# One matmul over the high and low parts of 240 tokens in five projections of a float32 hybrid decoder layer

## What is computed

```python
xn = rmsnorm(x, g1)
q, k, v, o, ig, fg, u, vb, ga, gb = split_in(xn @ w_in)
h, C, n, m = mlstm_branch(q, k * DK_A ** -0.5, v, ig, log_sigmoid(fg), C, n, m)   # chunks of 128
y_a = (sigmoid(o) * h) @ w_a
y_b = spatial_gate(gelu(u), rmsnorm(gelu(vb), g_v), w_s, b_s) @ w_b
x = x + (sigmoid(ga) * y_a + sigmoid(gb) * y_b) @ w_o
up = rmsnorm(x, g2) @ w_up
a, gval = split(causal_conv(up), 2)
x = x + (silu(a) * gval) @ w_down
y = rmsnorm(x, g_final)
```

## Time and profile before

| | |
|---|---|
| median of 3 runs | 938.73 us |
| range of the runs | 938.55 to 939.69 us |
| span of the profiled execution (first to last instruction) | 936.5 us |
| its own time beside the span | not listed apart; the median lies 2.2 us above the span |
| TensorE busy | 912.5 us, 97%, 7432 matmul records |
| weight loads busy | 900.9 us, 96% |
| VectorE busy | 524.1 us, 56% |
| ScalarE busy | 365.3 us, 39% |
| POOL busy | 136.6 us, 15% |
| mean DMA rate | 106 GB/s |

### The profile page before, as it was taken

How to read it: one execution, slowest core, us unless ns; L and a number is a source line. 1 busy time by engine, 2 the same in 40 slices (tenths; PEclk the granted TensorE clock), 3 DMA queues, 4 the chain that set the end, 5 groups by cost and what they waited for, 6 DMA issues and landing times.

```text
span 936.5 us, 19633 instructions
## 1 busy us (share of the span) xinstructions
PE 912.5 (97%) x7432; PEld 900.9 (96%) x7432; DVE 524.1 (56%) x802; ACT 365.3 (39%) x550; POOL 136.6 (15%) x180
## 2 busy tenths in 40 slices
PE   7999999999999999999999999999999999999993
PEld 6999999999999999999999999999999999999993
DVE  7874565453685444433335787777777777332234
ACT  5562333443783332322223344444444444222230
POOL 1842000002261111000005610000000000000002
PEclk9999999999999999999999999999999999999997
DMA  4312233124683112252224222222222223323212
GB/s 182 135 69 90 91 112 135 50 90 152 211 304 126 67 67 88 86 185 91 90 90 118 90 79 101 90 90 90 90 90 90 90 90 95 104 83 98 86 62 91
DMA packets 30008, 99.10 MB, mean 106 GB/s; under 512 B 4480, under 2 KB 6560, under 8 KB 29848
## 3 DMA queue, kind: packets, MB, share of 16 engines
q1 hardware_dynamic: 28528, 93.46, 28.2%
q0 software_dynamic: 1152, 4.66, 1.7%
q10 hardware_dynamic: 296, 0.55, 0.2%
HBM read 91.32 MB, written 7.34 MB: 105 GB/s over the span
## 4 chain that ended last, share of the span: by engine, by line
PE 88%; DVE 4%; POOLq 3%; issue 2%; DVEq 1%; DMA 1%; POOL 1%; ACT 0%; ACTq 0%
PE out L1286 81%; PE aux L1286 3%; PE trp L1286 2%; POOLq L1263 2%; DVE xl L780 1%; POOLq L1261 1%; PE trp L1315 1%; DVE wlo L738 1%; DVE y L1151 1%; DMA cwb<-in_conv_wb 0%; DMA gains<-in_gains 0%; PE aux L1421 0%; DVE ftmp L1147 0%; DVEq L831 0%; DVE mmax L816 0%
## 5 line engine op out<-in xcount | busy, mean ns | idle before, releaser
L738 DVE TENSOR_TENSOR wlo<-raw,whi 128x1024 fp32r<-128x1024 f32 (+1 forms) x149 | 187.1, 1256 | 226.1 <-ACT whi L408 225.9
L408 ACT ACTIVATE whi<-raw 128x1024 fp32r<-128x1024 f32 (+1 forms) x149 | 156.5, 1050 | 267.5 <-PE out L1286 265.7
L1286 PE MATMUL out<-xh,whi 128*128 128x260 f32 x864 | 178.9, 288 | 2.0 <-DVE wlo L738 2.0
L1286 PE MATMUL out<-xh,wlo 128*128 128x260 f32 x864 | 173.9, 283 | 0.0
L1286 PE MATMUL out<-xl,whi 128*128 128x260 f32 x864 | 173.7, 282 | 0.0
L1286 PE MATMUL out<-x2h,wlo 128*128 128x260 f32 x704 | 141.9, 283 | 0.0
L1286 PE MATMUL out<-x2h,whi 128*128 128x260 f32 x704 | 141.8, 282 | 0.0
L1286 PE MATMUL out<-x2l,whi 128*128 128x260 f32 x704 | 141.7, 283 | 0.0
L1286 PEld LDWEIGHTS out<-xh,whi 128*128 128x128 f32 x864 | 133.4, 188 | 2.9 <-DVE wlo L738 2.4
L1286 PEld LDWEIGHTS out<-xh,wlo 128*128 128x128 f32 x864 | 133.1, 188 | 0.0
L1286 PEld LDWEIGHTS out<-xl,whi 128*128 128x128 f32 x864 | 133.1, 188 | 0.0
(11 more groups left out here) (255 smaller groups left out, 1278.1 us busy)
## 6 DMA issues: line engine op xcount, KB each, us to landing
raw<-in_w_slots SPq DMA_DIRECT2D x125, 512.0 KB, 3.2
raw<-in_w_dn SPq DMA_DIRECT2D x16, 448.0 KB, 3.2
c_ring<-in_C_state SPq DMA_DIRECT2D x8, 512.0 KB, 4.6
row<-scratch SPq DMA_DIRECT2D x8, 512.0 KB, 5.4
out_C_sample<-c_ring SPq DMA_DIRECT2D x8, 512.0 KB, 3.9
raw<-in_w_dn SPq DMA_DIRECT2D x8, 512.0 KB, 3.6
xres<-in_x_all POOLq DMA_DIRECT2D x1, 2080.0 KB, 10.7
x<-in_x_all SPq DMA_DIRECT2D x3, 520.0 KB, 5.5
```

The costliest lines, as they stand in the source:

```text
L408: return act.activation(out, in_, func, **kw_)
L738: TT(wlo[p][:, 0:width], raw[p][:, 0:width], whi[p][:, 0:width].bitcast(F32), ALU.subtract)\
L1286: return pe.matmul(*a, **k)
```

## The change

In Q, K, V, WO and DN (`twin=True`) the high weights take the low and the high part of tokens 0 to 239 in one matmul of 480 columns. The low part's product so lands beside the high part's in the bank, not on it, and is added when the bank is emptied (`cross`). All tiles, the others too, now cut the tokens at 240, and put them so that the 520 results lie in one run across both banks. High and low parts get one tensor with a common stride for this. In Q, K and V ScalarE's copy signals `q_copied`, `k_copied` or `v_copied`; VectorE adds the crossed 240 columns and signals `evac`. In WO and DN VectorE does a second add after a drain. `mid` of K and V tiles moves from k = 3 to k = 5.

```diff
+CUT = 240
...
+        def tokens(bank):
+            return bank[:, :, :].rearrange("p a b -> p (a b)")[:, 512 - CUT:512 - CUT + TOK]
+        def cross(bank):
+            return bank[:, 0, 512 - 2 * CUT:512 - CUT]
...
-                A(both(qT[:, j, :]), out2(n)).then_inc(evac[n.c % 2], 1)
+                A(qT[:, j, :], out2(n)).then_inc(s_qc, 1)
...
-                A(both(ftmp[h % 2][:, :]), out2(n), scale=DK ** -0.5).then_inc(evac[n.c % 2], 1)
+                A(ftmp[h % 2][:, :], out2(n), scale=DK ** -0.5).then_inc(s_kc, 1)
...
+            def q_cross(j):
+                dve.wait_ge(s_qc, j + 1)
+                TT(qT[:, j, 0:CUT], cross(out_ps[(S_Q + j) % 2]), qT[:, j, 0:CUT], ALU.add).then_inc(evac[(S_Q + j) % 2], 1)
             low(At(S_Q + 2))
+            q_cross(0)
...
                 if h >= 1:
                     k_side(h - 1)
                 low(At(S_K + h + 2))
+                dve.wait_ge(s_kc, h + 1)
+                front = ftmp[h % 2][:, 0:CUT]
+                STT(front, cross(out_ps[(S_K + h) % 2]), DK ** -0.5, front, ALU.mult, ALU.add).then_inc(evac[(S_K + h) % 2], 1)
...
             low(At(S_V + 2))
+            v_cross(0, 0)
...
-                    TT(both(x1[:, j, :]), out2(n), both(xres[:, j, :]), ALU.add).then_inc(evac[n.c % 2], 1)
+                    TT(x1[:, j, :], out2(n), xres[:, j, :], ALU.add)
+                    dve.drain()
+                    TT(x1[:, j, 0:CUT], cross(out_ps[n.c % 2]), x1[:, j, 0:CUT], ALU.add).then_inc(evac[n.c % 2], 1)
                     dve.drain()
                     dve.nop().then_inc(s_x1, 1)
...
-                        TT(x1[:, j, h], o[:, a, :], x1[:, j, h], ALU.add).then_inc(s_x2f, 1)
+                        m = TT(x1[:, j, h], o[:, h], x1[:, j, h], ALU.add)
+                        if a == 0:
+                            dve.drain()
+                            m = TT(x1[:, j, 0:CUT], cross(out_ps[bank]), x1[:, j, 0:CUT], ALU.add)
+                        m.then_inc(s_x2f, 1)
...
-                    for wt, x in ((whi[p], hi), (whi[p], lo), (wlo[p], hi)):
-                        for a in range(2):
-                            m = MM(o[:, a, 0:HALF], wt[:, w], x[:, k0 + k, a * HALF:(a + 1) * HALF],
...
+                    if twin:
+                        MM(both_, whi[p][:, w], x[:, :, 0:CUT], start=first, stop=last, skip_group_check=True)
+                    else:
+                        MM(front, whi[p][:, w], hi[:, 0:CUT], start=first, stop=False)
+                        MM(front, whi[p][:, w], lo[:, 0:CUT], start=False, stop=False)
+                    MM(back, whi[p][:, w], hi[:, CUT:TOK], start=first, stop=False)
+                    MM(back, whi[p][:, w], lo[:, CUT:TOK], start=False, stop=False)
+                    MM(front, wlo[p][:, w], hi[:, 0:CUT], start=False, stop=last, skip_group_check=twin)
+                    m = MM(back, wlo[p][:, w], hi[:, CUT:TOK], start=False, stop=last)
...
-                tile(At(S_K + h), xh, xl, mid=(lambda: k_side(h - 1)) if h >= 1 else None)
+                tile(At(S_K + h), of(x_hl), twin=True, mid_at=5, mid=(lambda: k_side(h - 1)) if h >= 1 else None)
```

More of the change, by code:

```diff
@@ L1128, in dn_tile @@
                         h = slice(a * HALF, (a + 1) * HALF)
-                        TT(x1[:, j, h], o[:, a, :], x1[:, j, h], ALU.add).then_inc(s_x2f, 1)
+                        m = TT(x1[:, j, h], o[:, h], x1[:, j, h], ALU.add)
[3 more added lines that the diff above has]
+                        m.then_inc(s_x2f, 1)
                     return
-                TT(both(x1[:, j, :]), o, both(x1[:, j, :]), ALU.add).then_inc(evac[bank], 1)
+                TT(x1[:, j, :], o, x1[:, j, :], ALU.add)
+                dve.drain()
+                TT(x1[:, j, 0:CUT], cross(out_ps[bank]), x1[:, j, 0:CUT], ALU.add).then_inc(evac[bank], 1)
                 dve.drain()
@@ L1286, in MM, with tile @@
                 return pe.matmul(*a, **k)
-            def tile(n, hi, lo, k0=0, nk=KT, bank=None, use=None, start=True, stop=True, mid=None, mid_at=3, each=None, end=None):
+            def tile(n, hl, k0=0, nk=KT, bank=None, use=None, start=True, stop=True, mid=None, mid_at=3, each=None, end=None,
+                     twin=False):
                 p = n.c % 2
@@ L1293, in tile @@
                     pe.wait_ge(evac[p if bank is None else bank], n.half(1) if use is None else use)
-                o = out_ps[p if bank is None else bank]
+                b = out_ps[p if bank is None else bank]
+                both_ = b[:, 0, 512 - 2 * CUT:512].rearrange("p (a t) -> p a t", a=2)
+                front, back = b[:, 0, 512 - CUT:512], b[:, 1, 0:TOK - CUT]
                 for k in range(nk):
@@ L1326, in vb_tile @@
                 n = At(S_VB + t, i, 2)
-                tile(n, xh, xl, each=each, mid_at=5, mid=lambda: transposes(At(B_VB + t - 1, i, 2), n.plus(-1)))
-            tile(At(S_GATE), xuh, xul, each=s_xu)
-            tile(At(S_VB), xuh, xul)
+                tile(n, of(x_hl), each=each, mid_at=5, mid=lambda: transposes(At(B_VB + t - 1, i, 2), n.plus(-1)))
+            tile(At(S_GATE), of(xu_hl), each=s_xu)
+            tile(At(S_VB), of(xu_hl))
             pe.wait_ge(s_tri, 1)
-            tile(At(S_VB + 1), xuh, xul, end=lambda: transposes(At(B_VB), At(S_VB)))
+            tile(At(S_VB + 1), of(xu_hl), end=lambda: transposes(At(B_VB), At(S_VB)))
             vb_tile(1, 0, each=s_xn)
@@ L1446, in norm_sums @@
                 m.then_inc(signal, 1)
[L1448 to L1449 removed]
+            tile(At(S_UP), of(x2_hl), each=s_x2, mid_at=5, mid=lambda: norm_sums(s_acc, 1, s_ss2))
+            tile(At(S_UP + 1), of(x2_hl))
             with pe.Fori(1, FT) as i:
                 for t in range(2):
[L1452 removed]
+                    tile(At(S_UP + t, i, 2), of(x2_hl))
             def dn_pair(i, first=False):
@@ L1460, in dn_pair @@
                         pe.wait_ge(s_al, FT - 1 if q < 2 else FT)
-                    tile(n, acth, actl, k0=DN_CUTS[q], nk=DN_CUTS[q + 1] - DN_CUTS[q], bank=bank,
-                         use=At(S_DN + t, i, 2).half(1), start=q == 0, stop=q == 2)
+                    tile(n, act_of, k0=DN_CUTS[q], nk=DN_CUTS[q + 1] - DN_CUTS[q], bank=bank,
+                         use=At(S_DN + t, i, 2).half(1), start=q == 0, stop=q == 2, twin=True)
             dn_pair(0, True)
```

115 lines of the change are left out of this document (65 added, 50 removed).

## The result

The changed kernel takes **944.66 us** (median of 4 runs, 943.8 to 946.15), the kernel before, beside it, 938.99 (4 runs, 938.55 to 939.69): ratio **1.0064**, 95% interval 1.005 to 1.0078. It is slower by 5.7 us, where 931.0 was forecast and 943 was the upper end of the range. The profiled execution has a span of 942.1 us, 5.6 above that of before.

The account below looks back on a forecast made before the run. TensorE's matmul stream, busy 912.5 of 936.5 us, was taken as the bound. Terms -13.8 + 2.1 + 2.9 + 0.45 + 0.45 = -7.9 us gave 930.8 us, stated as 931; range 924 to 943 us, held at 0.80.

Parts of the forecast that it names:

- Step 1: Q, K, V, output projection and down: five matmuls for six in 368 k tiles, 37.5 ns each, -13.8 us.
- slow columns: Rival, all float32r matmuls: columns themselves cost 0.461 ns each, their count is unchanged, so nothing saved; 941.3 us, chance 0.12.
- the rival in which the change gives more: Rival, all tiles: 240 columns cost 111 ns, 25 us less, about 906 us; chance 0.05.
- Step 2: The other 808 k tiles, cut 240 and 280: 240 stays at 119.9 ns, 280 just at it; +2.1 us.
- third rival: Load and stream slow each other: 240 columns stay at 119.9 ns, 280 pay 128.2; 960 us, chance 0.15.
- Step 3: K and first V tiles: crossed add queued behind `low` makes TensorE wait 0.73 us in four rounds, +2.9 us.
- Steps 4 and 5: Second add after a drain, at output projection into up and at down's last tile: +0.45 us each.
- Step 6: Reads of 520 columns in one run instead of two, no DMA added or moved: costs nothing.

Follow-up runs that it names:

- the kernel at 256: The changed kernel with its tokens cut at 256 and 264 instead of 240 and 280, merged matmuls of 512 columns: 941.86 us, ratio 1.0031.

## Why the prediction was wrong

The spans' sum, step by step, from the stages' first starts:

| step | forecast, us | measured, us |
|---|---|---|
| 1. five matmuls for six, 368 k tiles | -13.8 | -1.7 (4.7 ns each) |
| 2. new cut, 808 k tiles | +2.1 | +3.4 (4.2 ns each) |
| 3. waits in K and V | +2.9 | +2.7 |
| 4. WO into up | +0.45 | +0.45 |
| 5. the end | +0.45 | +0.47 |
| sum | -7.9 | +5.3 (spans: +5.6) |

**Step 1 failed, by 12 of the 13.2 us: the price of one matmul by its width.** I read 119.9 ns as a floor of load and matmul and gave the 480 columns 202.3 ns; they take 218.1, and 240 take 112. The 11.6 ns above 108.3 were 7 to 8 ns of slow columns and 4 of a charge per matmul. The rival "slow columns" (0.461 ns each, 941.3 us) had the mechanism, and 221 ns for 480 columns was the nearest of my marks; it had no floor under it and so priced the new cut at nothing. The 111 ns for 240 columns of the rival in which the change gives more came true too, but beside 202.3 and 119.0 ns for the wide ones. The rows against the floor were at hand: eight passes of 128 columns start 111 ns apart with full weight loads, so a floor of 119.9 was no property of the load; and the last pair ahead of the transposes is as slow with a short load next, which I gave to the rival and then not its weight. My neighbours for long streams were passes of plain float32, which take 215/257 = 0.84 ns a column: they can't show a limit that lies at 0.446.

**Step 2** was mis-sized: a 240 does not stay at 119.9 but falls to the true floor of about 112 and no further, while a 280 pays 129.6. On a straight line the two would cancel; they are 1.4 ns a pair short of it. That is the third rival's shape (the narrow ones gain less than the wide ones pay), with a floor of 111.7 for 119.9 and a price of 4.2 for 25 ns a k tile. Its mark was a 240 of 112.9 ns with the 280 at 128.3; measured were some 112 and 129.6. About 1 of the 4.2 ns belongs to the order of the matmuls, which I costed at nothing.

**Step 3** was right in its loop, and its sum came out right by luck. Middle to middle is 8.72 us (8.71 forecast). But TensorE's own work there is 8 x 0.716 + 2.53 = 8.26 us, not 7.98, so a round loses 0.46, four lose 1.8; the other 0.9 us come from the V tile whose `low` POOL holds up, of which I had written that the chain is short from V1 on. That `low` of 3.19 us stands in the trace of before. That the waits are VectorE's order is shown: the add ahead of `low` takes them away, in K, then in V.

**Steps 4 and 5** hold: TensorE waits 0.5 us for POOL ahead of the norm sums where it waited for nothing, and the end is 0.47 us longer.

**Step 6** holds as far as it was tried: two pieces are free, and the placement in one run changes nothing. But the order into the banks, which I didn't cost, is worth 1.5 us at 260 columns in the medians (937.19 against 938.66 beside it) and 2.3 from the first tile on.

The range had a slip of its own: 5 us below 930.8 is 925.8, not 924. Nothing hangs on it, as the result lies above the upper end.

The Trainium skill's rule ("TensorE: Matmul & The Clock Gate", section "Back-to-back issue gap": N / 2.4 + 2.5 ns), which the page calls the gap of an isolated matmul, made the change worth 0.9 us at the most and came nearer to a saved matmul's worth (2.5 ns, an estimate by that rule, against 4.7) than my 37.5 did. Its figure for a column does not hold in this stream: 232.9 ns for 512 float32r columns, where it gives 215.8.

## What to carry to other kernels

Find out what a matmul's time consists of before merging matmuls: two matmuls above the floor save only the charge per instruction (here 4 ns of 120 by the line, 1 to 2 ns a k tile in the kernel at 256), columns are not saved. Weigh that against what the merging adds elsewhere: here the fastest kernel has no merged matmul, only the six of before in another order. Two kinds of row tell a floor from slow columns, one with fewer columns and the same load and one with the same columns and a lesser load; a neighbour of another element type tells neither. An operation that releases a waiting engine belongs ahead of long work on its queue that is needed later, and a split of equal tiles should not leave one part under the floor.

## What had not been expected of the hardware

- float32r columns above the floor cost 0.446 ns each, not the 0.417 of one a cycle at 2.4 GHz, and how they are read sets the time: 260 columns take 112.5 ns when one column is repeated, 120 in a row, 233 with step 2 and 236 with step 4. The Trainium skill ("SBUF — State Buffer", section "Door 1: The DMA port swizzle") says that two accesses to a 16-byte line are enough for full bandwidth; step 2 of four bytes makes two, and costs double here, as step 4 does. The measurement decides for TensorE's moving operand, which that section does not name.
- Taking the high and the low part of the same tokens in succession, into the same bank, makes the kernel 0.2% faster than two banks in turn, at 260 columns; at 240 and 280 columns it doesn't (944.01 against 942.98 us).
- One subtraction of VectorE's stretches from 1.23 to 3.42 us under a POOL operation of 2.44 us that began 0.1 us before it.
